# Linear attention on one core: the last, short chunk's values in four column groups of the array, added by one small product

## What is computed

```python
def gla_mixer(h, w_in, w_a2, b_a, norm_g, w_out):
    u = h @ w_in                       # q, k, v, r (gate), a1 (low rank)
    glog = log_sigmoid(a1 @ w_a2 + b_a) / 16
    # per head, chunk by chunk: b = cumsum(glog)
    #   o = (q * exp(b)) @ S  +  att(q, k, decay) @ v
    #   S = exp(b_last) * S + (k * exp(b_last - b)).T @ v
    o = o * rsqrt(mean(o * o) + 1e-6) * norm_g
    return (o * silu(r)) @ w_out
```

## Time and profile before

| | us |
|---|---|
| median of 3 runs | 3546.27 (3546.17 to 3559.31) |
| profiled execution | 3547.34 |
| its span | 3545.4 |
| PE busy in the span | 3366.9 (95%) |
| DVE busy | 1923.6 (54%) |
| ACT busy | 907.9 (26%) |

### The profile page before, as it was taken

The page is one execution under the profiler, slowest core; times in us unless marked ns, Lnnn a source line. Parts: engine busy times, 40 slices in busy tenths (PEclk is TensorE's granted clock), DMA queues, the critical chain, the costliest instruction groups (busy, mean ns, idle before and its releaser), DMA issues.

```text
span 3545.4 us, 57659 instructions
## 1 busy us (share of the span) xinstructions
PE 3366.9 (95%) x25645; PEld 2093.7 (59%) x25645; DVE 1923.6 (54%) x3171; ACT 907.9 (26%) x1850; POOL 51.2 (1%) x117
## 2 busy tenths in 40 slices
PE   6998879998999999889999999999999999999998
PEld 3445655558888888444444444445566447777753
DVE  2036763537676676655555550126988775444524
ACT  3005651115454554221010000100111413233310
POOL 2000000000000000000000000000000000000000
PEclk9999999999999999999999999999999999999999
DMA  6001002310000000331111112113011121100021
GB/s 242 0 0 56 1 24 72 120 58 3 18 18 4 4 4 17 115 113 65 48 59 48 45 60 80 43 59 98 24 36 36 62 76 54 36 24 24 1 89 65
DMA packets 110715, 177.24 MB, mean 50 GB/s; under 512 B 5443, under 2 KB 66626, under 8 KB 109826
## 3 DMA queue, kind: packets, MB, share of 16 engines
q1 hardware_dynamic: 101682, 144.67, 12.1%
q10 hardware_dynamic: 8784, 28.89, 2.3%
HBM read 147.33 MB, written 26.21 MB: 49 GB/s over the span
## 4 chain that ended last, share of the span: by engine, by line
PE 83%; DVE 9%; ACT 4%; DMA 2%; issue 1%; POOL 0%; ACTq 0%; DVEq 0%; SPq 0%; POOLq 0%
PE psum_all L66 82%; ACT sbuf_all L72 3%; DVE sbuf_all L91 3%; DVE sbuf_all L99 2%; DVE sbuf_all L81 2%; PE psum_all L111 1%; ACT L72 1%; DMA sbuf_all<-in_x 1%; DVE sbuf_all L105 1%; DVE sbuf_all L88 0%; DMA sbuf_all<-in_w_out 0%; DMA sbuf_all<-in_w_up 0%; DVE sbuf_all L111 0%; POOL sbuf_all L81 0%; DMA yd_spill<-sbuf_all 0%
## 5 line engine op out<-in xcount | busy, mean ns | idle before, releaser
L66 PE MATMUL psum_all<-sbuf_all 64*64 64x64 f32 (+8 forms) x24890 | 3270.0, 318 | 135.0 <-ACT sbuf_all L72 60.7
L66 PEld LDWEIGHTS psum_all<-sbuf_all 64*64 64x64 f32 (+3 forms) x24890 | 2010.7, 155 | 1370.7 <-issue 980.2
L72 ACT ACTIVATE sbuf_all<-psum_all 128x256 f32<-128x256 f32 (+6 forms) x889 | 363.9, 427 | 1457.6 <-PE psum_all L66 1316.7
L91 DVE SCALAR_TENSOR_TENSOR sbuf_all<-sbuf_all 128x520 f32<-128x520 f32 (+8 forms) x783 | 581.0, 776 | 16.9
L81 DVE TENSOR_TENSOR sbuf_all<-sbuf_all 128x640 f32<-128x640 f32 (+11 forms) x543 | 450.6, 853 | 134.2 <-ACT sbuf_all L72 91.3
L72 ACT ACTIVATE sbuf_all<-sbuf_all 128x64 f32<-128x64 f32 (+12 forms) x475 | 266.5, 574 | 821.5 <-DVE sbuf_all L75 349.1
L75 DVE COPY sbuf_all<-psum_all 128x256 f32<-128x256 f32 (+6 forms) x141 | 72.5, 524 | 473.4 <-PE psum_all L66 448.3
L72 ACT ACTIVATE sbuf_all<-psum_all,sbuf_all 128x1280 f32<-128x1280 f32 (+5 forms) x212 | 164.4, 781 | 313.5 <-PE psum_all L66 275.2
L81 DVE TENSOR_TENSOR sbuf_all<-sbuf_all,psum_all 128x512 f32<-128x512 f32 (+2 forms) x160 | 102.0, 639 | 250.6 <-PE psum_all L66 249.3
L105 DVE COPY_PREDICATED sbuf_all<-sbuf_all,psum_all 128x256 f32<-128x256 int32 (+2 forms) x296 | 144.0, 490 | 69.7 <-PE psum_all L66 64.1
L87 DVE TENSOR_SCALAR sbuf_all<-sbuf_all 128x256 f32<-128x256 f32 (+9 forms) x151 | 57.4, 417 | 162.6 <-ACT sbuf_all L72 159.4
(11 more groups left out here) (21 smaller groups left out, 167.6 us busy)
## 6 DMA issues: line engine op xcount, KB each, us to landing
sbuf_all<-in_w_mod SPq DMA_DIRECT2D x12, 2048.0 KB, 7.9
sbuf_all<-in_w_up SPq DMA_DIRECT2D x22, 1024.0 KB, 7.6
sbuf_all<-in_w_in SPq DMA_DIRECT2D x6, 2048.0 KB, 9.5
x_spill<-sbuf_all SPq DMA_DIRECT2D x16, 512.0 KB, 2.8
sbuf_all<-in_conv_w_in SPq DMA_DIRECT2D x16, 512.0 KB, 5.2
sbuf_all<-in_gla_w_in SPq DMA_DIRECT2D x8, 1024.0 KB, 5.3
sbuf_all<-in_w_down SPq DMA_DIRECT2D x4, 1792.0 KB, 7.5
hid_spill<-sbuf_all ACTq DMA_DIRECT2D x9, 512.0 KB, 2.6
```

The source lines that it names most:

```text
L66: return self.e.matmul(out, lhsT, rhs, start=start, stop=stop, skip_group_check=True)
L72: return self.e.activation(out, in_, func, bias=bias, scale=scale, **kw)
L91: return self.e.scalar_tensor_tensor(out, a, s, b, op0, op1) if self.e is not None else Unissued()
```

## The change

The last chunk's values of each head are made differently. The eight depth blocks of "v h 8" go to four column groups, 32 partitions of one bank each (two blocks accumulate in each), with the last 32 rows as the stationary operand instead of the last 16. ScalarE copies all 128x256 of it to `K.gla_parts`. A new step "sum_v h" multiplies `K.gla_parts` with a 128x16 matrix `K.gla_pick`, which has a one for each of the 16 wanted rows in each group, into another bank, and ScalarE copies the 16x256 to the values' place. `K.gla_pick` is made once by one reduction on VectorE from the identity. "sum_v h" is put into `filler` two places after the last value; the list of filler thereby is one longer for heads 0 to 3.

```diff
@@ gla_schedule
         if h < GH:
             filler += [("v", h, i) for i in range(NCH)]
+            late = len(filler) + 2
         ...
+        if h < GH:
+            filler.insert(late, ("sum_v", h))
@@ gla_memory
+    K.gla_parts = K.level["lower"][:, 4:6, :].rearrange("p h n -> p (h n)")
+    K.gla_pick = K.level["lower"][:, 6, 0:16]
@@ gla_tensor
+            if i < NCH - 1:
+                bank = open_bank(K, te, "v", h, i)
+                product(te, bank[0:m, 0:GV], lambda k: h1T(k, i * P, i * P + m), lambda k: w[:, k, :], KD).then_inc(*T.tick("v", h, i))
+            else:
+                bank = open_bank(K, te, "last_v", h)
+                for k in range(KD):
+                    g = slice(32 * (k % 4), 32 * (k % 4) + 32)
+                    done = te.matmul(bank[g, 0:GV], h1T(k, L2 - 32, L2), w[:, k, :], k < 4, k >= 4)
+                done.then_inc(*T.tick("last_v", h))
+                K.gla_weights.end(("v", h), T.now())
+        elif kind == "sum_v":
+            h, = at
+            i, m = NCH - 1, gla_rows(NCH - 1)
+            te.wait_ge(*S.by("last_v", h))
+            te.wait_ge(*V.by("pick"))
             bank = open_bank(K, te, "v", h, i)
-            product(te, bank[0:m, 0:GV], lambda k: h1T(k, i * P, i * P + m), lambda k: w[:, k, :], KD).then_inc(*T.tick("v", h, i))
-            if i == NCH - 1:
-                K.gla_weights.end(("v", h), T.now())
+            te.matmul(bank[0:m, 0:GV], K.gla_pick, K.gla_parts).then_inc(*T.tick("v", h, i))
@@ gla_vector
     ve.wait_ge(*L.g.by("padded"))
+    ve.reduce(K.gla_pick, K.ident.rearrange("p (g n) -> p n g", n=32)[:, 16:32, :], ALU.add).then_inc(*V.tick("pick"))
@@ gla_scalar
         elif kind == "v":
             h, i = at
-            if i % 2 == 0:
+            if i == NCH - 1:
+                se.wait_ge(*T.by("last_v", h))
+                if h:
+                    se.wait_ge(*T.by("v", h - 1, i))
+                se.activation(K.gla_parts, K.bank.view("last_v", h)[:, 0:GV], ACT.Copy).then_inc(*S.tick("last_v", h))
+                K.bank.end(("last_v", h), S.now())
+            elif i % 2 == 0:
...
+        elif kind == "sum_v":
+            h, = at
+            i, m = NCH - 1, gla_rows(NCH - 1)
+            se.wait_ge(*T.by("v", h, i))
+            if h >= 2:
+                se.wait_ge(*T.by("chunk", h - 2, NCH - 1))
+            se.activation(K.gv[h % 2][0:m, i, :], K.bank.view("v", h, i)[0:m, 0:GV], ACT.Copy).then_inc(*S.tick("v", h))
+            K.bank.end(("v", h, i), S.now())
```

## The result

The changed kernel takes 3553.42 us against 3545.87 us (medians of 22 runs each), 7.6 us more. The ratio estimated from all these runs, which isn't that of the two medians, is 1.0027, with a 95% interval of 1.0015 to 1.0039: +9.6 us, from 5.3 to 13.8. The forecast was +6.0 us, 3552. So the change made the kernel slower by some 0.3%.

What follows compares the result with a forecast made beforehand. TensorE was taken to bound the heads, with VectorE only 1.5 us early. Order with the saved work gave +2.6 us and the clock +3.4, so +6.0 on 3546.27, about 3552 us; forecast 3549.5 to 3555, whole range 3543 to 3557.

Steps and rivals of the forecast that it cites:

- The bound: Heads 1 to 3: TensorE work sets the time while VectorE's results are ready; VectorE is 1.5 us early at level 5.
- Work on TensorE: Last value chunk of each head: 3.6 us becomes 1.05 plus 0.65 for the sum, saving 1.9 a head, 7.6 in all.
- The other estimate of 1.1 us: Last chunk's column groups: by a skill rule, about 3.2 times faster, 1.1 us; some 0.5 us less gain over four heads.
- Work elsewhere at nothing: VectorE's reduction, ScalarE's four copies, the extra banks and SyncE's loads cost nothing; sum_v finds its copy done.
- Order: Longer filler puts a value ahead of the decay (level 6 in head 3); waits 4.7, 4.1, 4.1, 0.4 us; net +2.6 us.
- The clock: Behind the new level 5 waits in heads 1 and 2 the granted clock falls, 1.7 us lost each: +3.4 us.
- rival 3: Low clock lasts: each fall in heads 1 and 2 costs two or three times 1.7 us; 3555.5 to 3559, chance 0.1.
- The total: Whole kernel: +6.0 us on the median 3546.27, about 3552; forecast 3549.5 to 3555, chance 0.55.
- The bound of 0.5%: What a measurement of this kernel can tell from no change: about 0.5%, 18 us; same 0.96, slower 0.03, faster 0.01.
- the clock doesn't fall behind both new waits: Rival 1, heads 1 and 2: waits come but not both clock falls; +0.9 to +4.3 us, 3547 to 3550.5, chance 0.2.
- VectorE takes up the shift: Rival 2, decay chain: shift absorbed or release misread, saving stands; 3538.7, or 3540 to 3544 us; chance 0.12.
- the groups don't run side by side: Last chunk's 16 instructions at 0.216 us plus the sum: 10 us on top, about 3558, chance 0.03.

Runs made afterwards that it cites:

- run with the old order: Changed kernel with the step list of the kernel before, sum_v not counted in the quotient: heads' part 455.5 us, whole kernel 3541.98 us, ratio 0.999.
- both with the late decay: Decay h+1 moved behind decays h, in the changed kernel (heads' part 446.1 us, ratio 0.9964) and in the kernel before (453.3 us, 0.9988).
- run with the sum at once: Changed kernel with sum_v right behind the last value instead of two filler steps later: heads' part 475.5 us.
- run with the waits filled: Changed kernel with a useless 16-instruction product in each of the three long waits: heads' part 459.9 us, whole kernel 3547.67 us, ratio 1.0008.
- run with the order alone: Kernel before with one empty filler step per head where sum_v stands, no column groups: heads' part 464.8 us, whole kernel 3548.12 us, ratio 1.0014.

## Why the prediction was right, and which term was off

**The bound.** Right. TensorE alone sets the time where nobody is late, and VectorE was early by 1.5 us only. The run with the old order and both with the late decay move by what this says.

**Work on TensorE.** Right: 1.08 us a head for the groups against 1.05, and the pair for the sum 0.6 against 0.65. The other estimate of 1.1 us, for less than a fourfold speedup, is as near; 3.6 / 1.08 is 3.3, each with the last instruction's latency in it. The saving of 7.6 us over four heads showed as 7.2 once no wait hid it.

**Work elsewhere at nothing.** Right in the changed kernel: no wait of TensorE ended by ScalarE stands in it. The run with the sum at once shows what the two filler steps cover: 0.5 to 0.7 us.

**Order.** Right, and the reason for the result. Waits forecast at 4.7, 4.1, 4.1 and 0.4 us; the idle times are 4.74, 4.10 and 4.11, and 0.14 in head 3 (TensorE is busy for 4.16 of the 4.30 us up to level 7 at 3339.30). Idle time counts from the end of the last product's latency, some 0.2 us after the next could have started (an instruction of 256 columns takes 0.38 us and the next begins 0.22 after it), so each delay is that much longer than its idle time. The working put the decay of heads 1 and 2 at 3.46 us later; it came 3.4 later in head 1.

**The clock.** The mechanism was right, the size was not: this is the mis-sized term. I took 1.7 us for each of heads 1 and 2 and nothing more in head 0, 3.4 together. The stretches above lose 3.0, 2.9 and 1.7, so 7.6, of which 1.7 was there before: 5.9, or 2.5 more than forecast; by the run with the waits filled it is 7.3 less 1.7, so 5.6, or 2.2 more. That is most of the difference between +6.0 and the trace's +8.8 us. The parts add up: TensorE is idle 13.1 us against 3.15, so 9.9 more, with some 0.2 for each of the two new long waits, and 5.6 to 5.9 for the clock; less the 7.2 saved, this gives 8.7 to 9.0. I had the price from one wait, of 3.15 us. In heads 0 and 1 it came to nearly twice as much, as in rival 3, but no second wait was needed for it, and the waits of 7.51 us, which cost 1.9 and 2.7, speak against the length of the wait as its cause. What sets the length of the fall stays open.

**The total.** That the measured median lies 1.4 us from the forecast of 3552 is in part luck. The trace's +8.8 us on the forecast's own base, 3546.27, is 3555.1, at the very edge of its 3549.5 to 3555; the medians differ by 7.6 us and the ratio says 9.6. The bound of 0.5%, 18 us, on what can be told from no change was too wide as well: 22 runs of each told 0.3%.

**The rivals.** That the clock doesn't fall behind both new waits is ruled out by the trace; that VectorE takes up the shift, by the run with the order alone; that the groups don't run side by side, by the row of 64 instructions and the four under way at once. Rival 3 has a part of the truth: its price of two times 1.7 us is near what head 1 lost, 2.9, but not head 2, 1.7.

## What to carry to other kernels

Before taking work from the busiest engine, read how early the others are at its next waits: with 1.5 us of slack, a saving of 2.55 us gives back its excess as a wait, and what is saved must be paired with a move of the late chain. In a list of steps spread by a quotient, a new entry shifts all the others; put it in so that it isn't counted, and compare the order of the steps on each engine before the time. If a wait of some 4 us on TensorE can't be avoided, work that nobody needs can be cheaper than idling: filling the waits was worth 7.3 us here, since the clock stayed up. Better is to move the chain that it waits for, which was worth 21 us here.

## What the runs showed of the hardware

Sixteen fp32 instructions with 32 stationary columns in four column groups, 256 moving columns each, take about 1.08 us, 0.067 each, against 0.22 one after another.

Behind waits of 3.13 to 7.51 us in this stage the granted clock fell each time to 0.5, and the work that followed lost 1.7 to 2.9 us. How much did not go by the length of the wait: 4.74 us cost 2.9 in the changed kernel and 4.73 us 1.7 in the run with the sum at once; 4.10 and 4.11 us cost 2.9 and 1.7; 7.51 us cost 1.9 and 2.7. Behind waits of 0.52 to 1.95 us the clock stayed at 1.00. Why nearly equal waits are followed by different falls, and why both executions of the changed kernel fell the same way, I can't say from these runs. Nor did I follow the scatter of the stages ahead of this one, which is larger than all effects here.
